# One up row in four accumulated on VectorE in an encoder layer on one Trainium2 core

## The reference

```python
u_e = expert_down[expert]
act = jax.nn.gelu(jnp.einsum('chkd,cd->chk', u_e, xc,
                             preferred_element_type=jnp.float32), approximate=False)
v_e = expert_up[expert]
return jnp.einsum('chk,chkd->cd', (g * act).astype(xc.dtype), v_e)
...
f = _peer(h, w_query[l], sub_keys[l], expert_down[l], expert_up[l])
x = _layer_norm(DN_ALPHA * x + (1.0 + g_f) * f, ln2_g[l], ln2_b[l])
```

## Time and profile before

| | |
|---|---|
| median of 3 runs | 1824.02 us |
| profiled execution | 1825.07 us, its span 1823.3 us |
| busy: PE, DVE, ACT, POOL | 1473.1 (81%), 1116.8 (61%), 438.7 (24%), 983.7 (54%) us |
| DMA, mean over the span | 332 GB/s, 604.97 MB |
| L939, matmuls of the up rows | 2048 records, 1024.8 us |
| L1528, dots | 512, 622.8 us |
| L1163, diagonals | 512, 163.5 us |
| L681, gathers | 1024 issues |

### The profile page before, as it was taken

One profiled execution on the slowest core, in us unless ns is written; L12 is line 12 of the kernel. 1 busy time (PEld: TensorE's weight loads), 2 busy tenths in 40 slices (PEclk: granted clock), 3 DMA queues, 4 the chain that ended last, 5 costly groups with the idle time before them and its releaser, 6 DMA issues.

```text
span 1823.3 us, 14455 instructions
## 1 busy us (share of the span) xinstructions
PE 1473.1 (81%) x4072; PEld 684.6 (38%) x4072; DVE 1116.8 (61%) x2733; ACT 438.7 (24%) x1119; POOL 983.7 (54%) x1054
## 2 busy tenths in 40 slices
PE   6999988888988897766987988876787776776775
PEld 4444557534433553222432333422343322222222
DVE  5550367776666766676565667656455674577644
ACT  3111345322221322122222222212122121122111
POOL 1000000666666666666566666666676666667663
PEclk9999999999999999998899999999898999899999
DMA  9965402999999999999899999999999999999996
GB/s 308 380 236 112 162 4 46 338 366 356 371 355 392 407 373 366 368 366 364 310 359 409 378 366 376 373 358 373 376 360 357 374 361 383 372 348 374 374 378 244
DMA packets 190617, 604.97 MB, mean 332 GB/s; under 512 B 30897, under 2 KB 31305, under 8 KB 190379
## 3 DMA queue, kind: packets, MB, share of 16 engines
q0 software_dynamic: 147456, 536.94, 77.6%
q1 hardware_dynamic: 42027, 64.30, 10.5%
q10 hardware_dynamic: 1056, 2.82, 0.5%
HBM read 600.64 MB, written 3.34 MB: 331 GB/s over the span
## 4 chain that ended last, share of the span: by engine, by line
PE 34%; POOL 19%; issue 14%; DMA 13%; DVE 11%; another core or an unknown queue 6%; ACT 1%; SPq 1%; DVEq 0%; POOLq 0%; ACTq 0%
PE pair L939 17%; POOL big L681 14%; PE pair L691 9%; POOL region_v L681 5%; DMA big<-in_expert_up,expert_idx 5%; DMA region_v<-in_expert_up,expert_idx 3%; DVE big L1528 3%; PE pair L753 3%; DMA big<-in_expert_down,expert_idx 2%; DMA region_v<-in_expert_down,expert_idx 2%; PE pair L779 1%; DVE region_v L1528 1%; PE pair L718 1%; SPq L519 1%
## 5 line engine op out<-in xcount | busy, mean ns | idle before, releaser
L939 PE MATMUL pair<-big 128*128 128x512 f32 x1460 | 728.7, 625 | 196.7 <-DMA big<-in_expert_up,expert_idx 93.3
L1528 DVE CUSTOM_DVE_ANT_0 big<-big,pair 128x1024 f32<-128x1024 f32 x363 | 441.2, 1219 | 267.0 <-DMA big<-in_expert_down,expert_idx 176.6
L939 PEld LDWEIGHTS pair<-big 128*128 128x128 f32 x1460 | 267.2, 196 | 576.2 <-issue 550.7
L681 POOL DMA_INDIRECT big<-in_expert_up,expert_idx x365 | 346.2, 949 | 247.7 <-remote 106.8
L681 POOL DMA_INDIRECT big<-in_expert_down,expert_idx x363 | 346.4, 954 | 123.6 <-issue 101.7
L939 PE MATMUL pair<-region_v,big 128*128 128x512 f32 x588 | 296.1, 625 | 78.9 <-DMA region_v<-in_expert_up,expert_idx 35.9
L1528 DVE CUSTOM_DVE_ANT_0 region_v<-region_v,pair 128x1024 f32<-128x1024 f32 x149 | 181.6, 1219 | 109.9 <-DMA region_v<-in_expert_down,expert_idx 75.2
L1163 ACT ACTIVATE big<-ident,big 128x128 f32<-128x128 f32 x512 | 163.5, 390 | 354.6 <-issue 185.4
L939 PEld LDWEIGHTS pair<-region_v,big 128*128 128x128 f32 x588 | 106.5, 196 | 228.2 <-issue 216.7
L681 POOL DMA_INDIRECT region_v<-in_expert_up,expert_idx x147 | 139.3, 947 | 95.4 <-issue 36.4
L681 POOL DMA_INDIRECT region_v<-in_expert_down,expert_idx x149 | 140.6, 944 | 52.1 <-issue 42.1
(11 more groups left out here) (156 smaller groups left out, 1078.1 us busy)
## 6 DMA issues: line engine op xcount, KB each, us to landing
big<-in_w_ada SPq DMA_DIRECT2D x8, 2048.0 KB, 22.3
big<-in_w_in SPq DMA_DIRECT2D x5, 2048.0 KB, 13.1
big<-in_w_ada SPq DMA_DIRECT2D x16, 512.0 KB, 11.9
big<-in_w_query SPq DMA_DIRECT2D x4, 2048.0 KB
big<-in_expert_up,expert_idx POOLq DMA_INDIRECT x365
big<-in_expert_down,expert_idx POOLq DMA_INDIRECT x363
big<-in_w_out SPq DMA_DIRECT2D x2, 2048.0 KB
big<-na_scr SPq DMA_DIRECT2D x24, 128.0 KB, 4.1
```

The source lines that it names most:

```text
L681: nc.gpsimd.indirect_dma_start(places[place], None, (expert_down if kind == "down" else expert_up)[0], bass.IndirectOffsetOnAxis(expert_id ...
L939: last = nc.tensor.matmul(pair[t % 2][:, s * HALF:(s + 1) * HALF], diag[:, j, :], places[place][:, s * HALF:(s + 1) * HALF], start=(h == 0 ...
L1528: v.tensor_tensor_reduce(out=places[place], in0=places[place], in1=u_cur[:, :], scale=1.0, scalar=0.0, op0=ALU.mult, op1=ALU.add, accum_ou ...
```

## The change

From set 128 on, the sets with `at % 4 == 1` (96 of them) are *vector sets*. For these PE has no matmul and ACT makes no diagonal. Instead DVE takes the up row from its place, times the token's weight, and adds it to an accumulator of 128x1024 in SBUF: `mix_t` (1024 columns of `big`) for tiles 0 and 2, `mods[:, 0, :]` for 1 and 3. A tile's first vector set writes the accumulator by one tensor_scalar, the others add by scalar_tensor_tensor. The operation for set s stands behind the dot of set s+9 (VECTOR_LAG), and the last two, of sets 505 and 509, behind the last weigh. A place with a vector set's up row is released by vector_up_done instead of up_done. At a tile's end DVE multiplies the accumulator by (1 + gate), adds ALPHA times x into it ahead of the wait for PE, and adds it to PE's sums behind that wait. GATHERS and PLACE_OF are as before.

```diff
+SHARED_FROM, SHARED = 128, 1
+VECTOR_LAG = 9
...
+def on_vector(at):
+
+    return at >= SHARED_FROM and at % QUARTER == SHARED
+
+
+def tensor_sets(at):
+
+    return sum(not on_vector(i) for i in range(at))
...
                 if kind == "down":
                     pool.wait_ge(dot_done, at + 1)
+                elif on_vector(at):
+                    pool.wait_ge(vector_up_done, vector_sets(at + 1))
                 else:
-                    pool.wait_ge(up_done, at + 1)
+                    pool.wait_ge(up_done, tensor_sets(at + 1))
...
-                pe.wait_ge(diag_done, at + 1)
-                pe.wait_ge(place_in_use[place], 16 * USES["up", at])
-                for s in range(2):
...
+                if not on_vector(at):
+                    pe.wait_ge(diag_done, tensor_sets(at + 1))
+                    pe.wait_ge(place_in_use[place], 16 * USES["up", at])
+                    for s in range(2):
...
                     at = head * TOPK + j
+                    if on_vector(at):
+                        continue
...
+            accs = [mix_t.rearrange("p k s -> p (k s)"), mods[:, 0, :]]
...
+            def vector_up(at):
+
+                t, k, j = HEAD_AT[at // TOPK][0], at // TOPK % 2, at % TOPK
+                place, acc, weight = PLACE_OF["up", at], accs[t % 2], weights[:, k, j:j + 1]
+                if at == first_shared[0]:
+                    dve.wait_ge(pe_group, INDEX[("out", (TILES - 1, 1))] + 1)
+                dve.wait_ge(weight_done, at // QUARTER + 1)
+                dve.wait_ge(place_in_use[place], 16 * USES["up", at])
+                if at == first_shared[t]:
+                    v.tensor_scalar(acc, places[place], weight, None, ALU.mult).then_inc(vector_up_done, 1)
+                else:
+                    dve.wait_ge(vector_up_done, vector_sets(at))
+                    v.scalar_tensor_tensor(out=acc, in0=places[place], scalar=weight, in1=acc,
+                                           op0=ALU.mult, op1=ALU.add).then_inc(vector_up_done, 1)
+
             def residual(t):
 
-                dve.wait_ge(up_done, (POS_OF[t, PEER_HEADS - 1] + 1) * TOPK)
+                acc, past = accs[t % 2], (POS_OF[t, PEER_HEADS - 1] + 1) * TOPK
                 if t > 0:
                     dve.wait_ge(y_ready, t)
+                dve.wait_ge(vector_up_done, vector_sets(past))
+                link(v.tensor_tensor(acc, acc, mods[:, 3, :], ALU.mult))
+                v.scalar_tensor_tensor(out=acc, in0=x_sb[:, t, :], scalar=ALPHA, in1=acc,
+                                       op0=ALU.mult, op1=ALU.add).then_inc(acc_scaled, 1)
+                dve.wait_ge(acc_scaled, t + 1)
+                dve.wait_ge(up_done, tensor_sets(past))
...
-                link(v.scalar_tensor_tensor(out=sums, in0=x_sb[:, t, :], scalar=ALPHA, in1=sums,
-                                            op0=ALU.mult, op1=ALU.add))
+                link(v.tensor_tensor(sums, sums, acc, ALU.add))
...
+                    if at >= VECTOR_LAG and on_vector(at - VECTOR_LAG):
+                        vector_up(at - VECTOR_LAG)
...
             weigh(HEADS - 1, QUARTER - 1)
+            for at in range(SETS - VECTOR_LAG, SETS):
+                if on_vector(at):
+                    vector_up(at)
             residual(TILES - 1)
```

17 lines of the change are left out of this document (11 added, 6 removed).

## The result

The changed kernel takes **1829.16 us** (median of 20 runs, 1824.51 to 1837.47), the kernel before, measured beside it, 1824.06 us (20 runs, 1817.2 to 1834.42). Forecast were 1830.0 us, 1812 to 1850. The profiled execution took 1826.39 us, its span 1824.5.

The account below looks back on a forecast made before the run. From set 128 on the bound was taken to be how fast the DMA side takes gathers, with PE and DVE beside it. Against 1825.07 us, -4 + 6 + 4 - 1 = +5 gave 1830 us, range 1812 to 1850.

Parts of the forecast that it names:

- The bound: From set 128 on the DMA side's rate of taking gathers sets the pace, POOL 0.19 us ahead on each.
- The removed work, -4 for the knot: PE's 187 us less save nothing in the stream, but 4 us at 850 to 880 us, where PE decides.
- The load of DVE, 0 on the path: DVE gets 122 us of new operations, about 812 of 1095 us busy; 0 while dots stay within their places.
- The holds of POOL, +6: Two-SBUF-operand operations of DVE lengthen POOL's issues, 96 x 0.5 = 48 us, of which 6 us come through.
- The 12%: Share of POOL's longer issues that reaches the time: 0.11 of 0.93 us between two cycles of 24 issues.
- Rival A: POOL's holds are not absorbed, about 48 us come through: 1873 us; chance 0.10.
- The places, +4: With 12 places up to about 1093 us, two episodes of late DVE cost 4 us; with 20 places nothing.
- The end, -1: Without set 509 PE's last sets take 1.8 us less; the last row may keep some: -1 us.
- C: Rival: the relief of PE counts, knot gone wholly, holds and places cost nothing: 1814 us; chance 0.15.
- B: Rival: places run out, DVE is over 5 us late oftener than twice: 1848 us; chance 0.20.
- D: Rival: PE's clock falls and POOL waits for PE, two knots of 10 us: 1850 us; chance 0.05.

Follow-up runs that it names:

- Load alone: Kernel before plus 94 DVE operations nobody waits for, one operand in PSUM, one in SBUF; 1822.84 us against 1814.06, ratio 1.0053.
- load and holds: Kernel before plus 94 DVE operations of 128x1024 with two SBUF inputs that nobody waits for; 1828.47 us, ratio 1.0027.
- eleven in sixteen left out: Kernel before without PE's matmuls and ACT's diagonals for 264 of the 384 sets from 128 on, nothing on DVE instead; 1827.4 us, ratio 1.0028.
- removed work alone: Kernel before without matmuls and diagonals of the 96 vector sets, nothing on DVE instead; 1827.43 us, ratio 1.0012.
- places released at once: Changed kernel, operation reads a fixed tensor, vector row's place free once the row has landed; 1817.1 us against 1814.06, ratio 1.0018.
- PSUM operand, first time: Changed kernel, operation reads the token's vector in PSUM in place of the accumulator, rows not summed; 1856.66 us, ratio 1.0169.
- 104 sets from 304 on: Changed kernel with two vector sets in every four, but only from set 304 on; 1817.53 us against 1814.06, ratio 1.0018.
- one dot earlier: Changed kernel with VECTOR_LAG 8 instead of 9; 1829.4 us, ratio 1.0029.
- twice the sets: Changed kernel with 192 vector sets, two in every four from set 128 on; 1843.26 us, ratio 1.0107.
- twice the sets, PSUM: Changed kernel with 192 vector sets, each operation reading the token's vector in PSUM in place of the accumulator; 1842.05 us, ratio 1.0107.
- one operand: Changed kernel, each operation a tensor_scalar that overwrites the accumulator, rows not summed; 1836.96 us, ratio 1.0078.
- PSUM operand, second time: Changed kernel with the operation reading the token's vector in PSUM, repeated on another chip; 1849.82 us against 1814.06, ratio 1.0206.

## Why the prediction was right, and where its reasons were not

**The bound: right, as far as the runs go.** From 708 to 1803 us POOL issued 759 gathers before and 761 after (its count in the windows) at 367 and 368 GB/s, and neither a quarter nor two thirds of PE's sets less made the kernel faster. The DMA side sets the pace, POOL lies ahead of it, and the long waits on remote are that lead being given up. They shrank by 64 us, more than the 46 by which the issues grew.

**The removed work, -4 for the knot: not confirmed.** The run without that work gives +2.2 (-2.7 to +7.1), which doesn't hold -4. The knot did get milder: from 850 to 880 us the trace after moves 338 GB/s instead of the 281 of the earlier trace rows, and DVE's 8.57 us on ACT are 2.24. But the clock there is still 0.66, and in the stream as a whole it fell from 0.95 to 0.84. Whether the one makes up for the other no run shows.

**The load of DVE, 0 on the path: wrong, and this is the step that failed.** Its size was right: L1526 takes 1.28 us, 92 of them, and DVE is 73% busy in the stream (796 of 1095 us), where 812 was forecast. "On the path: 0, as long as the dots stay within their places" took no account of two things. Weights and indices come from DVE too, and PE's places hang on the weights. (This is how the code is; which of the two carries the loss was not measured.) And DVE has idle time only on the mean: it stands still for 3 to 7 us again and again, and with 27% idle instead of 37% it needs longer to catch up. By itself the load costs +9.6 us (6.3 to 12.9), a possible price of its PSUM operand included, and it doubles DVE's share of the chain that ended last, from 11 to 22%.

**The holds of POOL, +6: the size was right, the price wrong.** 96 x 0.5 = 48 us were forecast and 46 measured. But of these nothing came through that a run could find. Load alone cost +9.6 (6.3 to 12.9), load with holds +4.9 (1.8 to 8.0), on different chips. That less came with holds than without is itself not explained. The 12% was read from two cycles that differed by 0.11 us, and that was too fine a reading to carry a term. Rival A, the same holds unabsorbed, has nothing for it.

**The places, +4: of the right order, for partly wrong reasons.** Releasing them at once gives 2.4 us back, not clear of zero, and one dot of lag less gives nothing. Waits of POOL on L1526 from 708 to 1093 us are 6.6 + 2.8 + 1.4 = 10.8 us, within the few to 15 that the text allowed. But another 16.4 us (8.7 + 6.1 + 1.6) fell after 1190 us, where the prediction charged nothing, since it reckoned 16.6 us of margin:

```profile
POOL big L702 <- DVE big L1526: 8.7, 2, 4.9
...
POOL big L702 <- DVE mods L1526: 6.1, 1, 6.1
...
POOL region_v L702 <- DVE big L1526: 1.6, 1, 1.6
```

What such waits cost there is little, by the run from set 304 on, and more in the earlier stretch, by the runs with 192 sets.

**The end, -1: the wrong sign, in the one execution that shows it.** DVE waited 1.64 us for PE's last products where it waited 8.70, since the two operations and the sum with x now fill that time:

```profile
1813.09 1.29 DVE L1542 TENSOR_TENSOR big<-pair,mods 128x512 f32<-128x512 f32 x2 [1.64 <-PE pair L961]
```

From the end of the last issue (1802.82) to this operation it is 10.3 us; before it was 8.3 (1803.52 to 1811.83). PE's last 16 records ran from 1805.95 to 1812.98, 7.03 us where they took 7.21, but they began later. So the shorter wait came as forecast and brought no gain, but a loss of 2 us in this one execution.

**The sum.** By the runs: load and holds +4.9, the places +2.4, and the relief of PE what is left to the change's +5.7, -1.6, which is as uncertain as all three; measured alone the relief was +2.2, with -1.6 inside its interval. The prediction had +6, +4, -4, -1. That the total came out right was luck in this: a term of which no run finds anything (the holds, +6) stood where one belonged that was put at 0 (the load, +4.9 to +9.6), and they have about the same size. The rivals: C and A fell. B, a DVE later than thought, is nearest to what happened, at a quarter of its price (its 1848 is +24). D's falling clock is there, 0.84, but its knots and its 1850 are not; that the clock eats the gain of the relief is a reading of two runs and not shown.

```profile
861.00:872.00 11.00, 10.91 (x12) 3.50 (x12) 2.23 (x4) 2.32 (x5) 5.36 (x6) 0.50 0.73 238
```

## What to carry to other kernels

Where the DMA side sets the pace, as here, moving work from a busy engine to a less busy one gained nothing, and loaded the engine on which the release of the buffers hangs. Ask not how much idle time that engine has on the mean, but how long its longest standstill is and how many buffers cover it, and look at its share of the chain that ended last. Slower issues of an engine that runs ahead cost nothing that could be found, as long as its long waits were there to pay for them. And a forecast that comes true is no proof of its terms: only runs that carried less than all of them (load without holds, load and holds without late places) gave reason to think that two were swapped.

## What the runs showed of the hardware

**Which operations hold POOL.** Summed over the 1024 issues of a profile, the busy time of the gathers was 972.5 us before and 1017.0 with the change. It was 1019.7 with the 94 operations of two SBUF operands, 971.8 with the 94 that had one operand in PSUM, and 993.3 with the one-operand tensor_scalar: 44 us more with the change, then 47, none, and 21. "GPSIMD Engine Reference" of the Trainium skill, section "Key points", names instructions of VectorE with two SBUF inputs, or in a 2-port mode, as what contends. The first agrees with these numbers. The tensor_scalar took 0.79 us for its 1024 elements where the others took 1.22 to 1.28, and held POOL by 0.2 us each; whether it ran in such a mode no run here shows.

```profile
L1526 DVE TENSOR_SCALAR big<-big 128x1024 f32<-128x1024 f32 x36 | 28.4, 788 | 0.0
...
L702 POOL DMA_INDIRECT big<-in_expert_down,expert_idx x363 | 353.6, 974 | 120.9 <-issue 104.0 <-DVE expert_idx L1345 5.7 <-DVE big L1574 5.4
```

**Standstills of DVE that nothing explains.** Ahead of one step of `choose` (number 5 counted from 0; L1291 before, L1315 after, L1306 in the runs that leave sets out; one 128x256 addition on DVE's own results) DVE stands for 4 to 7 us in some heads. From 708 to 1803 us, remote and issue together, beside the profiled execution's own time less the median of before in its batch:

| kernel | L1315 stands, us | times | profiled execution |
|---|---|---|---|
| eleven in sixteen left out | 26.8 | 6 | -0.4 us |
| removed work alone | 14.4 | 6 | +0.3 |
| before | 24.3 | 5 | +1.0 |
| the change | 24.3 | 5 | +2.3 |
| load alone | 21.7 | 7 | +4.5 |
| places released at once | 19.9 | 5 | +6.6 |
| PSUM operand, first time | 30.0 | 6 | +7.3 |
| 104 sets from 304 on | 17.1 | 5 | +7.7 |
| one dot earlier | 31.4 | 8 | +9.5 |
| load and holds | 17.3 | 5 | +9.6 |
| twice the sets | 28.9 | 9 | +11.6 |
| twice the sets, PSUM | 76.3 | 13 | +15.3 |
| one operand | 38.9 | 12 | +20.9 |
| PSUM operand, second time | 78.1 | 16 | +33.3 |

The rows of the last (waits of DVE, 708 to 1803 us):

```profile
DVE big L1315 <- remote: 62.3, 13, 6.8
...
DVE big L1315 <- issue: 15.8, 3, 6.8
```

The two profiles of one and the same program say most: 6 standstills and 1831.95 us the one time, 16 and 1847.34 us the other. Their distances from before, 7.3 and 33.3 us, differ by 26 us and these standstills by 48, so what lies beyond the load's price in that program goes with them, not with the price of its operations. Below +10 us the table shows no such order, and it counts one line alone. (Its other runs took 1847 to 1858 us, so the profile at 1831.95 was its exception.) What makes the standstill frequent isn't settled. It is not the PSUM operand or the lack of holds alone: 94 such operations in the kernel before left it at 21.7 us. One guess was that the engine waits for its next instructions, which come by DMA beside the gathers (the page after lists 31 and 45 transfers of the kind instruction). The trace speaks against it. In the second profile of the PSUM operand, the four standstills of DVE between 1496 and 1518 us have no such transfer beside them: one begins at 1470.26 us and the next at 1518.54. Of the 16 standstills ahead of L1315, 3 meet one, about as many as chance would give (an estimate from 40 transfers in the 1103 us from 700 to 1803). So the cause stays open. For the same reason the runs without holds that were slower than the change (one operand, PSUM operand) don't show that holds help, nor by themselves that they are free; for that the load alone is the run to go by.
